# Prompt attention: the copy of the summed values out of PSUM is shared between ScalarE and VectorE

## The reference, cut to what matters

```python
def _mla_attend(q_lat, q_rope, ckv, kr, mask):
    s = (jnp.einsum('bqhl,bkl->bhqk', q_lat, ckv) + jnp.einsum('bqhr,bkr->bhqk', q_rope, kr)) * MLA_SCALE
    if mask is not None:
        s = jnp.where(mask, s, NEG_INF)
    p = jax.nn.softmax(s, axis=-1)
    return jnp.einsum('bhqk,bkl->bqhl', p, ckv)

def _swa_attend(q, k, v, sinks, key_mask):
    s = jnp.einsum('...qkgd,...skd->...kgqs', q, k) * SWA_SCALE
    ...
    p = jax.nn.softmax(jnp.concatenate([s, sink], axis=-1), axis=-1)[..., :-1]
    return jnp.einsum('...kgqs,...skd->...qkgd', p, v)

x = layer_norm(ALPHA * x + mix @ w_out)
x = layer_norm(ALPHA * x + (silu(x @ wg) * (x @ wu)) @ wd)
```

## Time and profile before

| | us |
|---|---|
| median of 3 executions | 3324.21 |
| lowest and highest | 3323.04 and 3330.74 |
| the profiled execution, its own time | 3323.04 |
| its span, first to last instruction | 3321.2 |
| stage B, layer 0 | about 245 to 536 of the span |
| stage B, layer 1 | about 1871 to 2188 of the span |

### The profile page before, as it was taken

The page is one execution under the profiler, slowest core; times in us unless marked ns, Lnnn a source line. Parts: engine busy times, 40 slices in busy tenths (PEclk is TensorE's granted clock), DMA queues, the critical chain, the costliest instruction groups (busy, mean ns, idle before and its releaser), DMA issues. The chain is left out here.

```text
span 3321.2 us, 46150 instructions
## 1 busy us (share of the span) xinstructions
PE 3064.4 (92%) x18240; PEld 2785.5 (84%) x18240; DVE 1508.7 (45%) x2841; ACT 885.0 (27%) x1710; POOL 860.3 (26%) x688
## 2 busy tenths in 40 slices
PE   7968887998999999999879688879999999999997
PEld 6946665887999999999879466658789999999996
DVE  6757776653222222222545577766532222222225
ACT  3323334435111111111223233344351111111111
POOL 2313334431111111111422133344212121111114
PEclk9979998999999999999989799979999999999998
DMA  4321104443111111110232211045331111111101
GB/s 163 132 65 42 33 26 156 151 131 106 45 44 38 44 38 44 38 38 25 103 103 91 75 33 33 23 156 172 113 116 39 44 38 44 38 38 38 38 25 71
DMA packets 129041, 231.68 MB, mean 70 GB/s; under 512 B 37744, under 2 KB 78960, under 8 KB 128592
## 3 DMA queue, kind: packets, MB, share of 16 engines
q1 hardware_dynamic: 118336, 198.80, 18.4%
q0 software_dynamic: 10576, 31.14, 2.4%
HBM read 175.46 MB, written 50.38 MB: 68 GB/s over the span
## 5 line engine op out<-in xcount | busy, mean ns | idle before, releaser
L2388 PE MATMUL PS<-xh,fwh 128*128 128x390 f32 (+1 forms) x2112 | 719.2, 341 | 2.0 <-DVE fwl L2294 1.3
L2389 PE MATMUL PS<-xl,fwh 128*128 128x390 f32 (+1 forms) x2112 | 720.5, 341 | 0.0
L2390 PE MATMUL PS<-xh,fwl 128*128 128x390 f32 (+1 forms) x2112 | 719.3, 341 | 0.0
L2336 DVE TENSOR_TENSOR acc<-acc,PS 128x390 f32<-128x390 f32 (+1 forms) x432 | 241.9, 560 | 420.6 <-PE PS L2390 420.6
L2314 DVE TENSOR_TENSOR gate<-PS,gate 128x390 f32<-128x390 f32 x132 | 74.4, 564 | 738.1 <-PE PS L2390 738.1
L2388 PEld LDWEIGHTS PS<-xh,fwh 128*128 128x128 f32 x2112 | 398.1, 189 | 5.2 <-DVE xl L2238 2.5
L2389 PEld LDWEIGHTS PS<-xl,fwh 128*128 128x128 f32 x2112 | 397.6, 188 | 0.3
L2390 PEld LDWEIGHTS PS<-xh,fwl 128*128 128x128 f32 x2112 | 397.6, 188 | 0.0
L2388 PE MATMUL PS<-hidh,fwh 128*128 128x390 f32 (+1 forms) x1056 | 358.2, 339 | 5.2 <-DVE hidl L2318 4.5
L2390 PE MATMUL PS<-hidh,fwl 128*128 128x390 f32 (+1 forms) x1056 | 359.5, 340 | 0.0
L2389 PE MATMUL PS<-hidl,fwh 128*128 128x390 f32 (+1 forms) x1056 | 357.9, 339 | 0.0
(11 more groups left out here) (440 smaller groups left out, 5428.3 us busy)
## 6 DMA issues: line engine op xcount, KB each, us to landing
raw<-in_W_FF SPq DMA_DIRECT2D x88, 512.0 KB, 3.2
fraw<-in_W_FF SPq DMA_DIRECT2D x44, 512.0 KB, 3.3
sqt_scratch<-sqTs POOLq DMA_DIRECT2D x18, 512.0 KB, 4.0
hc<-out_H SPq DMA_DIRECT2D x18, 512.0 KB, 3.6
out_H<-yo POOLq DMA_DIRECT2D x18, 512.0 KB, 3.0
dkraw<-in_CKVT SPq DMA_DIRECT2D x16, 520.0 KB, 4.6
QS<-sqt_scratch SPq DMA_DIRECT2D x16, 512.0 KB, 3.4
mt<-mix_scratch SPq DMA_DIRECT2D x16, 512.0 KB, 4.6
```

The source lines that it names most:

```text
L2336: dve.tensor_tensor(a, a, Tb[e % 2][:, 0:NT[i]], ALU.add).then_inc(S("f_y"), 1)
L2388: pe.matmul(out, wh, mh, start=start, stop=False)
L2389: pe.matmul(out, wh, ml, start=False, stop=False)
L2390: return pe.matmul(out, wl, mh, start=False, stop=stop)
```

## The change

In `ox`, ScalarE keeps the copy of head 0, and VectorE gets the copy of head 1. Both wait for what the pair waited for. The one semaphore `b_ox` becomes two, `b_ox_even` and `b_ox_odd`, and TensorE waits for both, ahead of the first `pv` of a pass and ahead of `ot`. What is computed stays the same.

```diff
@@ ScalarE, ox
                         if x >= 1:
                             act.wait_ge(S("b_item"), by_pe(l, ITEM["ot", x - 1]))
-                        for h in range(2):
-                            ins = act.activation(out_turned(x, h), out_sums(x, h), ACT.Copy)
-                        ins.then_inc(S("b_ox"), 1)
+                        act.activation(out_turned(x, 0), out_sums(x, 0), ACT.Copy).then_inc(S("b_ox_even"), 1)
@@ VectorE, behind sp
+                    elif k == "ox":
+                        x = u["x"]
+                        dve.wait_ge(S("b_pv"), F(l, "pv", u["n"]) + 1)
+                        if x >= 1:
+                            dve.wait_ge(S("b_item"), by_pe(l, ITEM["ot", x - 1]))
+                        dve.tensor_copy(out_turned(x, 1), out_sums(x, 1)).then_inc(S("b_ox_odd"), 1)
@@ TensorE, pv
                             if st["x"]:
-                                pe.wait_ge(S("b_ox"), F(l, "ox", st["x"] - 1) + 1)
+                                pe.wait_ge(S("b_ox_even"), F(l, "ox", st["x"] - 1) + 1)
+                                pe.wait_ge(S("b_ox_odd"), F(l, "ox", st["x"] - 1) + 1)
@@ TensorE, ot
-                        pe.wait_ge(S("b_ox"), F(l, "ox", x) + 1)
+                        pe.wait_ge(S("b_ox_even"), F(l, "ox", x) + 1)
+                        pe.wait_ge(S("b_ox_odd"), F(l, "ox", x) + 1)
```

## The result

| | before | after |
|---|---|---|
| median of 5 executions each, us | 3330.7 | 3356.3 |
| lowest and highest, us | 3323.0 and 3337.1 | 3350.4 and 3362.1 |
| the profiled execution and its span, us | 3323.0, 3321.2 | 3353.5, 3351.7 |
| mean granted clock of the profiled execution | 0.959 | 0.952 |

The ratio after to before is 1.0065, 95% interval 1.0046 to 1.0085. The forecast was 3333 us with a range of 3319 to 3343. The sign was right; the size was not, and the time lies outside the range. Over all executions of the two kernels on record (100 before, 22 after) the medians are 3331.1 and 3351.5: by these the change costs about 20 us, where the five and five above give 26.

The account below looks back on a forecast made before the run. In the prompt attention no engine was taken as saturated; VectorE's queue bounds places 2 and 4. Place costs less the end's gain made 4.8 us a layer, 9.6 in two, on 3323.0: 3333 us, range 3319 to 3343.

Parts of the forecast that it names:

- Duration and length of the copy: One copy on VectorE: 0.69 us long, the next instruction starting 0.61 to 0.72 later, taken as 0.63.
- Place 1: After an even window pass: the sums' banks are wanted later, so cost 0, at most 0.1 us; den waits about 0.1.
- Place 2: After an even head pass, VectorE bounds: 0.47 us three times a layer, 0.7 at the fourth, without mxs behind it.
- Place 3: After an odd window pass: TensorE's even head delayed, 0.4 us three times a layer; 0 at the fourth, hidden behind GpSimd.
- Place 4: After an odd head pass: VectorE has no cover, so 0.63 us three times a layer; the fourth is the stretch's end.
- End: End of each layer's prompt attention: two engines copy side by side while TensorE idles, minus 0.4 us per layer.
- ScalarE's relief: ScalarE's queue loses 0.48 us a place; gain 0 to 0.1 us at place 1, taken as 0, apart from the end.
- Distance from place 1 to place 1: From one place 1 to the next, the distance should grow by 0.47 + 0.4 + 0.63 = 1.5 us.
- Sum: Prompt attention: 1.4 + 0.7 + 1.2 + 1.9 - 0.4 = 4.8 us in one layer, 9.6 in two.
- The baseline: Whole program: the profiled execution of 3323.0 us, to which 9.6 was added; the median before was given as 3324.2.
- Rival 1: Longer pause at place 3 makes TensorE's clock fall more often: plus 7 us, 3340, at most 3343; chance 0.2.

Follow-up runs that it names:

- the two kernels with two fills: Unread matmuls in TensorE's pauses, four at place 1 and eight at place 3: on the kernel after 3331.1 us, on the kernel before 3319.7 us.
- the kernels with one place alone: Kernel before with VectorE copying head 1 only at place 2: 3346.3 us, 1.0048; or only at place 4: 3337.6 us, 1.0019.
- the one with all head passes: Kernel before with VectorE copying head 1 at the head passes only (places 2 and 4, and the last): 3348.8 us, 1.0058.
- the pause of before: Kernel after, but TensorE waits for VectorE's copy only ahead of head 1's matmuls, so place 3's pause is 2.15 us again: 3351.3 us, 1.0069.
- the row copy alone: Kernel before with one row's copy in front of place 4 moved from VectorE to ScalarE: 3335.3 us, ratio 1.0009.
- relieved VectorE: Kernel before with one row's copy moved to ScalarE, VectorE copying head 1 at the last pass alone, pauses at places 1 and 3 filled: 3310.5 us, 0.9914.

## Why the prediction was wrong, step by step

- *Duration and length of the copy*: 0.69 and 0.61 to 0.63 to the next start forecast; 0.686 in the median, and 0.61 at place 2 (2014.99 to 2015.60). Right.
- *Place 1, nothing*: right. The stretch 1 to 2 is the same at the same clock. den waits 0.26, where 0.1 was forecast.
- *Place 2, 0.47 and once 0.7*: 0.47 and once 0.52. Right, and the last one a little high: the wait of 0.19 for Pl was already there.
- *Place 3, 0.4, once 0*: 0.67 and once 0.57 to 0.72. Both too low, the first only by what the clock does. The 0.18 us of idle time should have hidden part, and at full clock it does: head 1 starts 1.05 us behind head 0 before (2009.54 to 2010.59) and 0.73 behind it after (1946.03 to 1946.76), so that of 0.67 only 0.35 is left, and with the pause filled the delay is 0.3 too. The 0.67 is read between stretches that have 6.8 us of half clock in both kernels, but not over the same matmuls. In three of the six stretches after, the clock fell within the pause, as at 2025.4; the three matmuls of head 0 then lasted 1.3 us (2026.27 to 2027.58), and GpSimd had been done before they were (its instruction ends at 2026.57). For the second term, I looked at head 0 alone. The copy also stands in front of VectorE's Ph of the *next* step, and GpSimd, which works without a gap there, waits for that Ph: its two instructions take 4.21 us from start to end in place of 3.62.
- *Place 4, 0.63*: 0.60. Right.
- *End, minus 0.4*: TensorE idle 0.83 in place of 1.17, minus 0.34. Right. ScalarE's relief gave nothing elsewhere, as forecast.
- *Distance from place 1 to place 1, 1.5*: with equal half clock, 0.47 + 0.67 + 0.60 = 1.7; at full clock 1.4.
- *Sum, 9.6*: the direct delays are 12.1 in two layers. A straight line through the 250 executions on record, with one slope for the clock and one level for each kernel, puts the kernel after at 12.2 us (plus or minus 1.4) over before at equal clock, and the two kernels with two fills at 10.1 and 0.2. At full clock, with 0.35 for each place 3, the direct sum is about 10, close to the 9.6 forecast. The line is a rough tool: the slope, 24 us for 0.01 of clock, is not the same everywhere, and for the kernels with one place alone it gives 4.8 (place 2) and -1.9 us (place 4) where the direct delays are 3.9 and 3.6, and for the one with all head passes 2.9 where they are 6.8.
- *The baseline*: I added the sum to one profiled execution of 3323.0 us at a clock of 0.959. The median before in the same comparison was 3330.7, and 100 executions run from 3320 to 3351. That execution was the fastest of the five: 7.7 us of the miss.
- *Rival 1, the clock falls more often*: this is what happened, beside the forecast and not in place of it. I gave it 0.2 and up to 10 us, as four to six more pieces of 3.4 us at up to 1.7 each. The profiled pair has 17.1 and 13.6 us more in the two layers, nine pieces, at about 1.1 each: some 10 us. Its mechanism as I wrote it, the pause at place 3 that is 0.6 longer, was at best a part: with the pause of before the half clock stayed, and in layer 0 four of the five added pieces stand behind place 1 and not behind place 3. Of the 23.3 us between 3333 and 3356.3, 7.7 are the baseline, 2.5 the direct delays and about 10 the added half clock in the stretch; the 3 that are left are not accounted for and are within the scatter. By the medians of all executions, 3331.1 and 3351.5, the clock's part is nearer 8.

The step that failed is the sum. It has the direct delays alone, 9.6 us on one execution of 3323.0, and holds the granted clock for a constant of the kernel, with rival 1 set beside it at a chance of 0.2. The runs show a second term, 8 to 13 us for more time at half clock, next to direct delays of 12.1 (about 10 at full clock). The time is above the range by this term and the low baseline together, and a little by the last place 3, put at nothing. The other direct terms were right to 0.2 us.

The Trainium skill, "TensorE: Matmul & The Clock Gate", section "HAM oscillation — how this bites in real kernels", says that the cost of falling back is paid at each repetition. The runs agree: in the kernel before the pieces at half clock come back behind each place 3, and with two pauses filled they are fewer (17.1 and 10.2 us in place of 23.9 and 23.9).

**Left open.** Why a shorter path (the row copy alone) got more half clock is not explained by any run; what sets the placing of the pieces was not tried by itself. Not tried either: a fill at place 1 alone, a fill of the pieces of 1.14, 1.46 and 0.81 us, and the relieved VectorE with both fills but without the shared last copy.

## What to carry over

Where TensorE is idle for a microsecond or two again and again (0.8 to 2.8 us here), treat the granted clock as a term of its own: for before and after, count the microseconds at 0.50 next to the distances between fixed points, and price a change at equal half clock. Moving half a microsecond onto an engine that bounds a stretch (VectorE here) because another one has time free is a loss, even if the busy shares look balanced. Matmuls that nothing reads, put into repeated pauses, are worth a try in more than one place: the longest pause alone gave nothing in the kernel before, that and the one at place 1 gave 0.4%, and together with a relieved VectorE 0.6 to 0.9%. And compare like with like: the kernel after with its pauses filled is as fast as the kernel before, but still 11 us behind the kernel before with the same fills.

## What was not expected of the hardware

- One kernel scatters by 0.9% from execution to execution (before: 3320 to 3351 us in 100), and the granted clock goes with it (0.950 for 3346.6 us, 0.958 for 3322.8 in the same comparison).
- The stretch 1 to 2 takes 18.98, 20.03, 21.25 or 22.77 us with 0, 3.4, 6.8 or 10.2 us at half clock: 0.31 to 0.37 us for each, although the clock is halved.
- The clock fell behind a pause that was filled (357.3 above), while the pause at place 1, 0.9 us, had been left open; with both filled and VectorE relieved it stayed at 1.00 for 276 us of layer 0 (256.8 to 533.3), over idle pieces of 1.14 and 0.81 us in each period.
